# Channel fold from reflected sums, and a new order of the transfers at the layer boundary, in a two-layer encoder kernel

## The chip, the cores and the metric

The kernel runs on all 8 cores of one Trainium2 chip, one batch row (4096 positions of width 1024) on each core. No core talks to another. The metric is the device time in microseconds of the slowest core.

## The reference, cut to what matters

```
def fourier_mixer(h, w_in, w_out):              # layer 0
    proj = h @ w_in
    xin, z = proj[..., :E], proj[..., E:]       # E = 2048
    xg = xin.reshape(b, s, 8, 256)
    y = fft2(xg, axes=(positions, group channels), norm="ortho").real
    return (y.reshape(b, s, E) * silu(z)) @ w_out

def sgu_mixer(h, w_in, ...):                    # layer 1
    u, v = gelu(first 2E columns of h @ w_in);  z = the last E columns
    v = layer_norm(v); v = per chunk of 128 positions: w_s @ v + b_s
    return (u * v * silu(z)) @ w_out

for each layer:  x = x + mixer(rms_norm(x))
return rms_norm(x)
```

## The kernel before, in words

Layer 0 turns the order of the Fourier mixer round: the position transform is taken of the normed input (width 1024), and the channel transform is folded into the weights, so that one product per channel group gives the transformed branch. Layer 1 works on blocks of 512 positions.

**Opening (lines 446 to 521).** 32 steps, one tile of 128 positions each. SP loads x (`load_x`, up to 8 ahead in 6 buffers); ACT squares (`square`, L391); GpSimd makes the reciprocal root in two small operations (`norm`, L399 and L401); VectorE scales (L403); TensorE transposes (L481), applies the first part of the position transform (L491) and runs one group of gate columns (`zgroup`, L412, 8 matmuls). SP stores the intermediate U to DRAM. Two slices of fold weights (`load_wb`, 0 and 1) are loaded by GpSimd's queue in steps 12 and 14.

**Second transform (L551 to L584).** Eight steps `qd` from 7 to 0: SP has issued 32 loads of V; TensorE makes H (L558, L566), ACT and VectorE evict it (L545, L547). `fold(0)` runs in four parts, in steps 4 to 1. At the end GpSimd's queue issues loads of gate weights (`load_wz` 6 to 10) and fold weights.

**Groups g = 0 to 7 (L883 on).** `pq(g)` is 128 matmuls of 260 columns in eight steps, each evicted by ACT (`pc`, L269) and VectorE (L605, L608); `gate(g)` multiplies by the gate tiles `sz` (six of 8 KB a partition, used in turn) on VectorE (L626); `fold(g+1)` makes the weights `wp` for the next group; then `zall(zt)` makes further gate tiles, 64 matmuls each. A `tick()` after each of the 8 parts of `pq` and `zall` issues, by its count, a weight cast from DRAM to DRAM on GpSimd's queue (`casts`, 32 of 512 KB, the bf16 copies of layer 1's weights and of W0) or a store of a gated tile (`stores`, 1 MB on SP to `gy`). GpSimd's transfers cast f32 to bf16 on the way and land in the order of their queue.

`fold(g)` is, for each of 8 slices dc of the model width, two matmuls with 256 columns each, which add up over the two halves of the 256 group channels:

```
for kc in range(2):
    pe.op(lambda e: e.matmul(bank[:, h * 256:(h + 1) * 256],
                             wb[wb_slot(2 * g + kc)][0][:, dc * 128:(dc + 1) * 128], fmat[:, kc, :], ...
```

**Boundary (L907 to L980).** After the last `zall` SP loads the row tile `szsp`, W0 (two of 2 MB), three tiles of x (`load_x1`, 512 KB each) and `g1t` (512 KB). After `fold(6)` and `fold(7)`, `pq(6)` begins; `last_column` (L663) makes eight special rows, which GpSimd gates (L626 with GpSimd as its engine). SP then loads the even blocks of `gyt` (12 of the 16 channel blocks of the first 512 positions in two loads; blocks 12 to 15 are read from `sz` in place), stores the special rows (`gy<-szsp`), and loads the odd blocks. During `pq(7)` SP issues ring loads 1 to 4 (layer-1 weights, 1 MB each) and then ring 0, x tile 3 and the stores of blocks 12 to 15. TensorE goes on with `out0` (L751): 28 matmuls for position tile 0, 28 for tile 1, 4 for tile 0, and so on, 128 in all for the first block. `residual` and `norm1` follow for each tile, ACT transposes the normed tile by DMA (`send1`, L177) and `vtile` (L821) starts layer 1. From there on each 512-position block repeats the same 2-stage pattern: `vtile`, `wide` (L848) with `mix` (L858: four matmuls of 128 columns, each with weights of its own), `out1` and `out0` (L751).

The order on each engine is the order of the program text. An operation waits only for semaphores that a small dependency tracker (`Q.deps`) sets, also for buffers that share an address range.

Of the kernel before, what the change touches and what calls it, by code (L numbers as in the profile page):

```python
# [19 lines left out]

def _chan_order():
    o = []
    for g in range(8):
        o += [g * 256 + m for m in range(128)]
        o += [g * 256 + 128] + [g * 256 + 256 - m for m in range(1, 128)]
    return np.array(o)

def _host_consts():
    bf = ml_dtypes.bfloat16
    c = np.arange(256)[:, None]  # L30
    m = np.arange(128)[None, :]
    ang = 2 * np.pi * ((c * m) % 256) / 256.0
    Fm = np.concatenate([np.cos(ang), np.sin(ang)], axis=1)
    Fm[:, 128] = np.cos(np.pi * np.arange(256))
    Fm = Fm.reshape(2, 128, 256).transpose(1, 0, 2)
# [31 lines left out]
    pk = np.concatenate([Fm.reshape(128, 512), rows(B64)], axis=1)  # L67
# [115 lines left out]
def build():  # L183
# [9 lines left out]
    wb_in = din("wbT", [16, 128, D])  # L193
# [11 lines left out]
    c_pk = din("c_pk", [128, 576], BF16)  # L205
# [10 lines left out]
    with ExitStack() as es:  # L216
# [82 lines left out]
        with ExitStack() as sa:  # L299
# [11 lines left out]
            def tile(name, shape, dtype, off=None):  # L311
# [3 lines left out]
            cpk, cpkb = tile("cpk", [128, 576], BF16)  # L315
            tr, trb = tile("tr", [128, 128], BF16)
            fmat = cpk[:, 0:512].rearrange("p (a b) -> p a b", b=256)
            b64 = cpk[:, 512:576]
# [29 lines left out]
            wb = [tile(f"wb{i}", [128, D], BF16, (top["at"] - 4096 if i < 2 else vh + 2048 * (i - 2)) + 2048 * (i % 2 if i < 2 else 0))  # L348
                  for i in range(6)]
# [4 lines left out]
            wsT, wsTb = tile("wsT", [128, 8, 128], BF16)  # L354
            assert top["at"] <= nc.sbuf_usable_end, (top["at"], nc.sbuf_usable_end)
# [8 lines left out]
            d_wb = [dsem(f"d_wb{i}") for i in range(6)]  # L364
# [12 lines left out]
            def wb_slot(i):  # L377
                return i if i < 2 else 2 + (i - 2) % 4

            def load_wb(i):  # L380
                k = wb_slot(i)
                pool.dma(wb[k][0][:], wb_in[i], d_wb[k], writes=[wb[k][1]])
# [41 lines left out]
            def fold(g, dcs):  # L424
                w_, wpb = wp[g % 2]
                for d2 in dcs:
                    bank, bb = next_f()
                    for h in range(2):
                        dc = 2 * d2 + h
                        for kc in range(2):  # L430
                            pe.op(lambda e: e.matmul(bank[:, h * 256:(h + 1) * 256],  # L431
                                                     wb[wb_slot(2 * g + kc)][0][:, dc * 128:(dc + 1) * 128], fmat[:, kc, :],
                                                     start=(kc == 0), stop=(kc == 1)),
                                  [wb[wb_slot(2 * g + kc)][1], cpkb], [bb], waw=False, inc=(h == 1 and kc == 1))
# [30 lines left out]
            norm(2)  # L465
            zq = []
            behind = []
            nxt = 6
            for s in range(32):
# [38 lines left out]
                if s in (12, 14):  # L508
                    load_wb(s // 2 - 6)
# [16 lines left out]
            stores = []  # L526
            late = []

            def tick():
# [3 lines left out]
                if stores and ticks["n"] % 4 == 0:  # L533
                    stores.pop(0)()
# [16 lines left out]
            for qd in range(7, -1, -1):  # L551
# [34 lines left out]
            def pq(g):  # L586
                w_, wpb = wp[g % 2]
                (Dt, Dtb), (St, Stb) = DS[g == 7]
                for qd in range(8):
# [21 lines left out]
                    if g == 7 and 0 < qd < NR:  # L611
                        load_ring(qd)
# [197 lines left out]
            def send1(n):  # L810
                j_, jb = xn1[n % 2]
                t = n % 4
                act.dma_t(h1T[:, :, t * 128:(t + 1) * 128], j_[:], d_t[t], [jb], [h1Tb[t]])

            def vtile(i, t):
                sm_, smb = sm[t]
                for j in range(4):
                    r_, rb = ring[(12 * i + j) % NR]
# [22 lines left out]
            def wide(i, k, ct, func, out_ap, wb_):  # L841

                n = 12 * i + 4 + 4 * k + ct // 4
                r_, rb = ring[n % NR]
# [38 lines left out]
            for g in range(8):  # L883
                pq(g)
                if g == 0:
# [3 lines left out]
                    load_wz(11)  # L889
# [43 lines left out]
            sp.dma(gsp[6:8], g67[:, :], d_67, reads=[g67b], writes=gyTb[13:16:2], waw=True)  # L933
# [102 lines left out]
def _in_maps(inputs):  # L1036
# [7 lines left out]
    base["wbT"] = np.ascontiguousarray(w_in0[:, :E].T).reshape(16, 128, D)  # L1044
# [17 lines left out]
```

How the kernel before makes its waits and increments, by code:

```python
    def wait(self, tok):  # L105
        if tok is None:
            return
        sem, val = tok
        if sem is self.sem and self.kind == "pe":
            return
        k = id(sem)
        if self.seen.get(k, 0) >= val:
            return
        self.eng.wait_ge(sem, val)
        self.seen[k] = val
# [32 lines left out]
    def op(self, fn, reads=(), writes=(), waw=True, cost=0.3, inc=True):  # L148
        self.load += cost
        self.deps(reads, writes, waw)
        inst = fn(self.eng)
        if inc:
            self.n += 1
            inst.then_inc(self.sem, 1)
            tok = (self.sem, self.n)
        else:
            tok = (self.sem, self.n + 1)
        self.mark(tok, reads, writes, waw)
        return tok
# [1 line left out]
    def dma(self, out, in_, dsem, reads=(), writes=(), waw=False, more=False, **kw):  # L161
        if not more and dsem.n > 0:
            self.wait((dsem.sem, dsem.n))
        self.deps(reads, writes, waw)
        self.eng.dma_start(out=out, in_=in_, **kw).then_inc(dsem.sem, 16)
        dsem.n += 16
        tok = (dsem.sem, dsem.n)
        self.mark(tok, reads, writes, waw)
        return tok
# [1 line left out]
    def dma_t(self, out, in_, dsem, reads=(), writes=()):  # L172
        if dsem.n > 0:
            self.wait((dsem.sem, dsem.n))
        self.deps(reads, writes, True)
        self.eng.dma_start_transpose(out=out, in_=in_).then_inc(dsem.sem, 16)
        dsem.n += 16
        tok = (dsem.sem, dsem.n)
        self.mark(tok, reads, writes, True)
        return tok
```

## Time and profile before

| what | us |
|---|---|
| three runs | 1580.16, 1621.85, 1579.46 (median 1580.16) |
| the profiled execution, its own time | 1582.04 |
| its span on the slowest core (core 1) | 1580.7 |
| spans of the eight cores | 1564.3 to 1580.7 |
| TensorE busy on core 1 | 1545.7 |
| VectorE, ACT, GpSimd busy on core 1 | 747.1, 515.9, 156.4 |

The span runs from the first to the last instruction of a core; the execution's own time is 1.3 us longer. Busy times are sums over instructions, and matmuls are pipelined, so that the time of one is longer than the distance to the next.

### The profile page before, as it was taken

Reading aid. Unit: us, or ns where it says so; the run is one execution under the profiler, and the core shown is the slowest. Engines: PE = TensorE matmul, PEld = TensorE weight load, DVE = VectorE, ACT = ScalarE, POOL = GpSimd, SP = SyncE. Lnnn points to the kernel's source line nnn. Section 1 sums busy time; section 2 is a strip of 40 time slices with the busy share of each in tenths; the row PEclk is TensorE's granted clock in tenths of the full one; section 3 lists DMA queues with packets and bytes.
Section 4 is the critical chain, followed back from the end, with each engine's and each line's share of the span. In section 5 each row is a group of like instructions: output and inputs, shape, how many; then the busy total and the mean of one; then the engine's idle time right before and its main releaser. Section 6 shows DMA issues by size and latency. Waiting matters only on the chain.

```text
span 1580.7 us, 25439 instructions; the slowest of 8 cores (1564.3 to 1580.7 us)
## 1 busy us (share of the span) xinstructions
PE 1545.7 (98%) x8458; PEld 782.7 (50%) x8458; DVE 747.1 (47%) x1245; ACT 515.9 (33%) x915; POOL 156.4 (10%) x336
## 2 busy tenths in 40 slices
PE   6999999999899999999999999999999999999997
PEld 3557766646644444544444444445444444544443
DVE  5866532213636435624553463356245435624552
ACT  5766333333223313322331232133123313322331
POOL 3311111010211011001000100110010011001000
PEclk9999999999999999999999999999999999999999
DMA  9986999999887941643453155335324531643411
GB/s 256 288 249 170 171 139 152 152 144 180 250 205 189 242 176 48 226 150 98 152 199 125 38 188 199 107 116 201 134 69 167 207 113 47 226 152 96 148 46 54
DMA packets 103298, 247.72 MB, mean 157 GB/s; under 512 B 40042, under 2 KB 56042, under 8 KB 87402
## 3 DMA queue, kind: packets, MB, share of 16 engines
q1 hardware_dynamic: 53652, 207.76, 39.8%
q0 software_dynamic: 15568, 29.63, 14.9%
q10 hardware_dynamic: 33952, 8.72, 3.3%
q8 instruction: 71, 1.16, 0.3%
q14 instruction: 55, 0.45, 0.1%
HBM read 225.24 MB, written 58.87 MB: 180 GB/s over the span
## 4 chain that ended last, share of the span: by engine, by line
PE 94%; DMA 4%; DVE 1%; issue 1%; ACT 0%; SPq 0%; POOL 0%; DVEq 0%; ACTq 0%; POOLq 0%
PE pf L848 28%; PE pf L751 27%; PE pf L412 14%; PE pf L821 14%; PE pf L595 5%; PE pf L858 2%; DMA gy<-sz_77 1%; DMA a0x_59<-xt 1%; DMA gyt<-gy 1%; PE pb L481 1%; PE pf L491 1%; PE pf L558 1%; DMA h1T<-xn_0_2525 1%; PE pf L431 1%; SPq L166 0%
## 5 line engine op out<-in xcount | busy, mean ns | idle before, releaser
L751 PE MATMUL pf<-W_2513,gyt 128*128 128x512 bf16 x992 | 219.2, 382 | 7.4 <-DMA gyt<-gy 7.4
L751 PE MATMUL pf<-W_2524,u 128*128 128x512 bf16 x1024 | 222.3, 379 | 0.0
L751 PEld LDWEIGHTS pf<-W_2513,gyt 128*128 128x128 bf16 x992 | 97.6, 98 | 126.6 <-issue 13.0
L751 PEld LDWEIGHTS pf<-W_2524,u 128*128 128x128 bf16 x1024 | 100.2, 98 | 120.8
L851 ACT ACTIVATE u<-pf 128x512 bf16<-128x512 f32 x128 | 76.5, 597 | 164.2 <-PE pf L848 154.7
L825 ACT ACTIVATE v<-pf 128x512 f32<-128x512 f32 x128 | 75.4, 597 | 121.1 <-PE pf L821 101.6
L848 PE MATMUL pf<-h1T,ring_2522 128*128 128x512 bf16 x416 | 96.8, 385 | 0.0
L848 PE MATMUL pf<-h1T,ring_2519 128*128 128x512 bf16 x416 | 96.5, 382 | 0.0
L848 PE MATMUL pf<-h1T,ring_2523 128*128 128x512 bf16 x416 | 95.5, 380 | 0.0
L848 PE MATMUL pf<-h1T,ring_2520 128*128 128x512 bf16 x416 | 94.9, 379 | 0.0
L848 PE MATMUL pf<-h1T,ring_2521 128*128 128x512 bf16 x384 | 88.3, 379 | 0.0
L605 DVE TENSOR_TENSOR Dt_93<-pc_97,pf 128x256 bf16<-128x256 f32 x28 | 11.8, 421 | 144.9 <-PE pf L595 120.8
L862 DVE SCALAR_TENSOR_TENSOR ytmp_2532<-pf,gTs,TT 128x512 f32<-128x512 f32 x64 | 48.1, 751 | 48.6 <-PE pf L858 48.5
L742 POOL TENSOR_SCALAR sm_2546<-sm_2546 128x1 f32<-128x1 f32 x24 | 5.3, 221 | 631.6 <-ACT sqj L787 588.0
L848 PEld LDWEIGHTS pf<-h1T,ring_2522 128*128 128x128 bf16 x416 | 40.1, 99 | 44.4 <-issue 5.2
L848 PEld LDWEIGHTS pf<-h1T,ring_2523 128*128 128x128 bf16 x416 | 39.8, 98 | 43.8 <-issue 1.5
L848 PEld LDWEIGHTS pf<-h1T,ring_2519 128*128 128x128 bf16 x416 | 39.8, 98 | 43.6 <-issue 3.5
L848 PEld LDWEIGHTS pf<-h1T,ring_2520 128*128 128x128 bf16 x416 | 39.6, 98 | 43.3 <-issue 0.3
L851 ACT ACTIVATE sg_2543<-pf 128x512 bf16<-128x512 f32 x64 | 38.2, 598 | 69.2 <-PE pf L848 58.9
L851 ACT ACTIVATE sg_2544<-pf 128x512 bf16<-128x512 f32 x64 | 38.2, 598 | 67.6 <-PE pf L848 64.4
L595 PE MATMUL pf<-H,wp_85 128*128 128x260 bf16 x512 | 58.3, 276 | 0.0
L595 PE MATMUL pf<-H,wp_84 128*128 128x260 bf16 x512 | 57.6, 274 | 0.0
(298 smaller groups left out, 2317.8 us busy)
## 6 DMA issues: line engine op xcount, KB each, us to landing
ring_2519<-wind SPq DMA_DIRECT2D x20, 1024.0 KB, 7.4
ring_2520<-wind SPq DMA_DIRECT2D x19, 1024.0 KB, 7.1
ring_2521<-wind SPq DMA_DIRECT2D x19, 1024.0 KB, 6.7
ring_2522<-wind SPq DMA_DIRECT2D x19, 1024.0 KB, 7.1
ring_2523<-wind SPq DMA_DIRECT2D x19, 1024.0 KB, 6.4
gyt<-gy SPq DMA_DIRECT2D x7, 2048.0 KB, 12.4
wind<-w_in1p POOLq DMA_DIRECT2D x24, 512.0 KB, 42.1
V<-ud SPq DMA_DIRECT2D x32, 256.0 KB, 7.9
```

The costliest lines, as they stand in the source:

```text
L412: pe.op(lambda e: e.matmul(bank[:], w[:, dc, :], hT[:, dc, hb * 512:(hb + 1) * 512], start=(dc == 0), stop=(dc == 7)), [wb_, hTb[hb], hTal ...
L431: pe.op(lambda e: e.matmul(bank[:, h * 256:(h + 1) * 256], wb[wb_slot(2 * g + kc)][0][:, dc * 128:(dc + 1) * 128], fmat[:, kc, :], start=( ...
L481: pe.op(lambda e: e.transpose(out=bank[:, dc * 128:(dc + 1) * 128], in_=xn_[:, dc * 128:(dc + 1) * 128], identity=ident[:]), [xnb, identb] ...
L491: pe.op(lambda e: e.matmul(bank[:], tr[:], xn_[:, h * 512:(h + 1) * 512], start=True, stop=True), [trb, xnb], [bb], waw=False)
L595: pe.op(lambda e: e.matmul(bank[:, 0:HQ], w_[:, dc, cs * 128:(cs + 1) * 128], H[:, qd, dc, cs, :], start=(dc == 0), stop=(dc == 7)), [wpb, ...
L751: pe.op(lambda e: e.matmul(bank[:], lhs(kc), rhs[:, kc, nh * 512:(nh + 1) * 512], start=(kc == 0), stop=(kc == 15)), lb(kc) + rb(kc), [bb] ...
L821: pe.op(lambda e: e.matmul(bank[:], h1T[:, dc, t * 128:(t + 1) * 128], r_[:, dc, :], start=(dc == 0), stop=(dc == 7)), [h1Tb[t], rb], [bb] ...
L825: act.op(lambda e: e.activation(out=vj, in_=bank[:], func=AF.Gelu_apprx_tanh), [bb], [vjb])
L848: pe.op(lambda e: e.matmul(bank[:], r_[:, dc, c0:c0 + 128], h1T[:, dc, :], start=(dc == 0), stop=(dc == 7)), h1Tb + [rb], [bb], waw=False, ...
L851: act.op(lambda e: e.activation(out=out_ap, in_=bank[:], func=func), [bb], wb_)
L858: pe.op(lambda e: e.matmul(bank[:, t * 128:(t + 1) * 128], vhat[t][0][:, ct * 128:(ct + 1) * 128], wsT[:, ct // 2, :], start=True, stop=True),
L862: dve.op(lambda e: e.scalar_tensor_tensor(out=y_[:].rearrange("c (t p) -> c t p", p=128), in0=bank[:].rearrange("c (t p) -> c t p", p=128) ...
```

## The change: what it does

Two parts.

1. The fold uses the symmetry of cosine and sine. The host pairs channel c with 256 - c (row 0 pairs 0 with 128) and lays the f32 weights out in pieces: 8 groups of 4 quarters of the model width, 128 partitions, 2 x 256 values, 256 KB each. SP loads a piece without a cast into a staging buffer (`st`, one or two slots), and GpSimd makes the sum and the difference of its two halves as bf16 (`eo`), two operations of 128 x 256 a piece, 64 in all. The fold is then one matmul of 129 columns with the sums and one of 192 columns with the differences, in place of two of 256. Pieces 0 to 3 pass in steps 8 to 24 of the opening, 4 and 5 are loaded in steps 28 and 29, 6 to 11 pass in the second transform, and the generator `sums()` moves 12 to 31, one step a tick, six ticks a piece, through one slot. `eo` 1 and 2 lie where gate weights 0 to 3 lie, so `load_wz` 6 and 7 go behind `fold(1)` and 8 and 9 behind `fold(2)`. The other `load_wb` are gone.
2. At the boundary SP holds back the three x tiles and `g1t` until `gyt` has landed; the stores of blocks 12 to 15 each wait for one of the four transposes of `send1`; the ring's slots are turned by one, so that loads 0 to 3 go out during `pq(7)` and load 4 after it.

The diff, cut to its core:

```
+_HARM = [*range(0, 128, 2), *range(1, 128, 2)]
...
+    FE = np.concatenate([np.cos(ang), np.cos(np.pi * c)], axis=1)
+    FE[0, 64:128] = 0.0
+    FO = np.zeros((128, 192))
+    FO[0, :64] = 1.0
+    FO[1:, 64:] = np.sin(ang[1:])
...
+            eo = [tile(f"eo{i}", [128, 2, D], BF16, o) for i, o in enumerate((top["at"] - 4096, wzo, wzo + 4096, vh + 4096, vh))]
...
+            st = [tile("st0", [128, 2, 256], F32, top["at"] - 2048), tile("st1", [128, 2, 256], F32, top["at"] - 4160)]
...
+            def load_piece(n):
+                t_, b_ = st[n % 2 if 4 <= n < 12 else 0]
+                sp.dma(t_[:], wb_in[n // 4, n % 4], d_st[n % 2 if 4 <= n < 12 else 0], writes=[b_], waw=True)
+            def sum_piece(n):
+                t_, b_ = st[n % 2 if 4 <= n < 12 else 0]
+                eo_, eob = eo_of(n // 4)
+                q = n % 4
+                for k, op in enumerate((ALU.add, ALU.subtract)):
+                    pool.op(lambda e: e.tensor_tensor(out=eo_[:, k, q * 256:(q + 1) * 256], in0=t_[:, 0, :],
+                                                      in1=t_[:, 1, :], op=op), [b_], [eob], waw=False)
+            folded = {"n": 0, "summed": 12}
+            def sums():
+                for n in range(12, 32):
+                    while n >= 20 and folded["n"] < n // 4 - 1:
+                        yield
+                    load_piece(n)
+                    for _ in range(4):
+                        yield
+                    sum_piece(n)
+                    folded["summed"] += 1
+                    yield
+                    yield
...
+                while folded["summed"] < 4 * g + 4:
+                    next(summing)
...
-                        for kc in range(2):
-                            pe.op(lambda e: e.matmul(bank[:, h * 256:(h + 1) * 256],
-                                                     wb[wb_slot(2 * g + kc)][0][:, dc * 128:(dc + 1) * 128], fmat[:, kc, :],
-                                                     start=(kc == 0), stop=(kc == 1)),
+                        for k, f, a, z in ((0, fE, 0, 129), (1, fO, 64, 256)):
+                            pe.op(lambda e: e.matmul(bank[:, h * 256 + a:h * 256 + z], eo_[:, k, dc * 128:(dc + 1) * 128], f,
+                                                     start=(k == 0), stop=True, skip_group_check=(k == 1)),
...
-                    if 0 < g < 6:
-                        load_wb(2 * g + 4)
-                        load_wb(2 * g + 5)
+                    folded["n"] = g + 1
...
-                if s in (12, 14):
-                    load_wb(s // 2 - 6)
+                if s in (12, 16, 20, 24):
+                    sum_piece(s // 4 - 3)
+                if s in (8, 12, 16, 20):
+                    load_piece(s // 4 - 2)
+                if s in (28, 29):
+                    load_piece(s - 24)
...
+            keep = {"n": 0}
...
+                next(summing, None)
+                if len(stores) > keep["n"] and ticks["n"] % 4 == 0:
                     stores.pop(0)()
...
+                for n in ((4,), (5, 6), (7,), (8,), (9,), (10,), (11,), ())[7 - qd]:
+                    sum_piece(n)
+                    if n < 10:
+                        load_piece(n + 2)
                 if qd == 0:
-                    load_wb(2)
-                    load_wb(3)
-                    for i in range(6, 9):
-                        load_wz(i)
-                    load_wb(4)
-                    load_wb(5)
-                    for i in range(9, 11):
-                        load_wz(i)
+                    load_wz(10)
...
                     if g == 7 and 0 < qd < NR:
-                        load_ring(qd)
+                        load_ring(qd - 1)
...
-                    k = n % NR
+                    k = (n + 1) % NR
...
                 act.dma_t(h1T[:, :, t * 128:(t + 1) * 128], j_[:], d_t[t], [jb], [h1Tb[t]])
+                if n < 4:
+                    sp.wait((d_t[t].sem, d_t[t].n))
+                    stores.pop(0)()
+                    if n == 3:
+                        sp.dma(gsp[6:8], g67[:, :], d_67, reads=[g67b], writes=gyTb[13:16:2], waw=True)
...
-                    load_wz(11)
+                    for i in (6, 7, 11):
+                        load_wz(i)
...
                 if g == 7:
-                    load_ring(0)
                     load_x1(3)
-                if g == 7:
-                    while stores:
-                        stores.pop(0)()
+                    load_ring(4)
...
+                if g == 1:
+                    for i in (8, 9):
+                        load_wz(i)
...
-                    for n in range(3):
-                        load_x1(n)
-                    sp.dma(g1t[:], g1.partition_broadcast(128), d_g1, writes=[g1b], waw=True)
...
                 if g == 6:
+                    keep["n"] = 4
...
                     sp.dma(gyt[:, 1:12:2, :], even[1, :, 0:6, 0:512], d_g, reads=gyTb[1:12:2], writes=[gytb], more=True)
+                    sp.wait((d_g.sem, d_g.n))
+                    for n in range(3):
+                        load_x1(n)
+                    sp.dma(g1t[:], g1.partition_broadcast(128), d_g1, writes=[g1b], waw=True)
```

## Rows read from the trace of the kernel before

**Rows 1.** The page: its head, and busy time by engine.
```profile
span 1580.7 us, 25439 instructions; the slowest of 8 cores (1564.3 to 1580.7 us)
PE 1545.7 (98%) x8458; PEld 782.7 (50%) x8458; DVE 747.1 (47%) x1245; ACT 515.9 (33%) x915; POOL 156.4 (10%) x336
```

**Rows 2.** Span and granted clock by core: core 3.
```profile
core 3: 1578.8 us, clock 0.990
```

**Rows 3.** Waits of TensorE on core 1: us in total, times, longest.
```profile
PE pf L751 <- DMA gyt<-gy: 7.4, 1, 7.4
```

**Rows 4.** Stretches of core 1: length, busy by engine, clock, DMA share, GB/s.
```profile
75.00:85.00 10.00, 10.00 (x72) 5.42 (x71) 9.47 (x13) 8.14 (x16) 2.91 (x7) 1.00 1.01 318
...
151.00:388.00 237.00, 237.00 (x1511) 147.75 (x1510) 70.78 (x231) 80.98 (x162) 34.48 (x55) 1.00 1.04 150
```

**Rows 5.** Chain that ended last, in order of time: start, us, what.
```profile
164.94 1.75 PE pf L431 x16
...
449.81 10.68 DMA h1T<-xn_0_2525
...
501.82 1.73 PE pf L848 x8
503.77 1.73 PE pf L848 x8
...
548.70 55.25 PE pf L751 x256
```

**Rows 6.** Timeline of core 1, 385 to 465 us: start, us, engine, line.
```profile
394.63 0.33 SPq L166 DMA_DIRECT2D gy<-sz_77  x1
...
398.74 8.73 POOL L626 TENSOR_TENSOR szsp<-p_100,szsp 8x2048 bf16<-8x2048 f32 x4 [53.16 <-ACT pc_97 L269]
...
407.22 14.35 PE L595 MATMUL pf<-H,wp_85 128*128 128x260 bf16 x128
...
413.38 0.29 SPq L166 DMA_DIRECT2D gy<-szsp  x1
...
415.91 0.39 SPq L166 DMA_DIRECT2D gyt<-gy  x1
...
428.92 4.57 PE L751 MATMUL pf<-W_2513,gyt 128*128 128x512 bf16 x12 [7.35 <-DMA gyt<-gy]
...
460.84 1.89 PE L821 MATMUL pf<-ring_2519,h1T 128*128 128x512 bf16 x8 [1.21 <-DMA h1T<-xn_0_2525]
```

**Rows 7.** Core 3: the last matmuls of `pq`, and the first of `vtile`.
```profile
405.96 14.35 PE L595 MATMUL pf<-H,wp_85 128*128 128x260 bf16 x128
...
L821 PE MATMUL pf<-ring_2519,h1T x224: 379/379/379, 455.7 to 1478.4; 128*128 128x512 bf16 x112
```

**Rows 8.** Transfers issued at 380 to 386 us: KB each, us to landing.
```profile
x_0_2515<-x SPq DMA_DIRECT2D x1, 512.0 KB, 17.9
...
g1t<-l_norm SPq DMA_DIRECT2D x1, 512.0 KB, 20.4
```

**Rows 9.** Groups by shape: GpSimd's largest product.
```profile
L626 POOL TENSOR_TENSOR szsp<-p_100,szsp 8x2048 bf16<-8x2048 f32 x1 | 4.1, 4072 | 53.2 <-ACT pc_97 L269 53.2
```

**Rows 10.** Timeline of core 1 near the opening's end.
```profile
98.57 0.57 POOL L401 TENSOR_TENSOR stats<-stats,mhalf 128x1 f32<-128x1 f32 x1 [0.21 <-POOL stats L399]
...
99.31 0.75 DVE L403 TENSOR_SCALAR a0xn_63<-a0x_55,stats 128x1024 bf16<-128x1024 f32 x1
...
101.34 0.61 PE L481 MATMUL pb<-ident,a0xn_63 128*128 128x128 bf16 x8
```

**Rows 11.** Transfers issued at 44 to 50 us, then at 166 to 172 us, to landing.
```profile
a0x_55<-xt SPq DMA_DIRECT2D x1, 512.0 KB, 7.2
...
wz_83<-wz POOLq DMA_DIRECT2D x1, 256.0 KB, 37.6
```

**Rows 12.** Stores and loads of SP: beside the casts, and in layer 1.
```profile
gy<-sz_73 SPq DMA_DIRECT2D x1, 1024.0 KB, 20.0
...
x_0_2515<-x SPq DMA_DIRECT2D x7, 512.0 KB, 3.7
```

More of the change, by code:

```diff
@@ L23, in _chan_order @@
     for g in range(8):
-        o += [g * 256 + m for m in range(128)]
-        o += [g * 256 + 128] + [g * 256 + 256 - m for m in range(1, 128)]
+        o += [g * 256 + m for m in _HARM]
+        o += [g * 256 + 128] + [g * 256 + 256 - m for m in _HARM[1:]]
     return np.array(o)
@@ L29, in _host_consts @@
     bf = ml_dtypes.bfloat16
-    c = np.arange(256)[:, None]
-    m = np.arange(128)[None, :]
+    c = np.arange(128)[:, None]
+    m = np.array(_HARM)[None, :]
     ang = 2 * np.pi * ((c * m) % 256) / 256.0
-    Fm = np.concatenate([np.cos(ang), np.sin(ang)], axis=1)
-    Fm[:, 128] = np.cos(np.pi * np.arange(256))
-    Fm = Fm.reshape(2, 128, 256).transpose(1, 0, 2)
+    FE = np.concatenate([np.cos(ang), np.cos(np.pi * c)], axis=1)
[3 more added lines that the diff above has]
+    FO[1:, 64:] = np.sin(ang[1:])
     TR = np.zeros((128, 2, 2, 32))
@@ L65, in rows @@
         return a.reshape(4, 32, -1).transpose(1, 0, 2).reshape(128, -1)
-    pk = np.concatenate([Fm.reshape(128, 512), rows(B64)], axis=1)
+    pk = np.concatenate([FE, np.zeros((128, 1)), FO, rows(B64)], axis=1)
     bdt = np.stack([rows(BD[pr]) for pr in range(32)], axis=1)
@@ L313, in tile @@
                 return t, Buf(name, (o, o + n))
-            cpk, cpkb = tile("cpk", [128, 576], BF16)
+            cpk, cpkb = tile("cpk", [128, 386], BF16)
             tr, trb = tile("tr", [128, 128], BF16)
-            fmat = cpk[:, 0:512].rearrange("p (a b) -> p a b", b=256)
-            b64 = cpk[:, 512:576]
+            fE = cpk[:, 0:129]
+            fO = cpk[:, 130:322]
+            b64 = cpk[:, 322:386]
             g0s, g0sb = tile("g0s", [128, 8], F32)
@@ L347, in build @@
             wp = [tile(f"wp{i}", [128, 8, 256], BF16) for i in range(2)]
-            wb = [tile(f"wb{i}", [128, D], BF16, (top["at"] - 4096 if i < 2 else vh + 2048 * (i - 2)) + 2048 * (i % 2 if i < 2 else 0))
-                  for i in range(6)]
+            eo = [tile(f"eo{i}", [128, 2, D], BF16, o) for i, o in enumerate((top["at"] - 4096, wzo, wzo + 4096, vh + 4096, vh))]
             bdt, bdtb = tile("bdt", [128, 32, 128], BF16, top["at"])
@@ L363, in build @@
             d_wz = [dsem(f"d_wz{i}") for i in range(6)]
-            d_wb = [dsem(f"d_wb{i}") for i in range(6)]
+            d_st = [dsem(f"d_st{i}") for i in range(2)]
             d_gy = [dsem(f"d_gy{i}") for i in range(6)]
@@ L375, in load_wz, with eo_of @@
                 pool.dma(wz[i % 6][0][:], wz_in[i], d_wz[i % 6], writes=[wz[i % 6][1]])
[L377 to L382, printed above, removed]
+            def eo_of(g):
+                return eo[g if g < 3 else 4 - g % 2]
+            def load_piece(n):
[20 more added lines that the diff above has]
+                    yield
             def load_x(t):
@@ L465, in build @@
             norm(2)
+            summing = sums()
             zq = []
@@ L532, in tick @@
                     next(casts, None)
-                if stores and ticks["n"] % 4 == 0:
+                next(summing, None)
+                if len(stores) > keep["n"] and ticks["n"] % 4 == 0:
                     stores.pop(0)()
@@ L817, in vtile @@
                 for j in range(4):
-                    r_, rb = ring[(12 * i + j) % NR]
+                    r_, rb = ring[(12 * i + j + 1) % NR]
                     bank, bb = next_f()
@@ L843, in wide @@
                 n = 12 * i + 4 + 4 * k + ct // 4
-                r_, rb = ring[n % NR]
+                r_, rb = ring[(n + 1) % NR]
                 c0 = (ct % 4) * 128
@@ L1043, in _in_maps @@
     base["wz"] = np.ascontiguousarray(wz.transpose(2, 1, 0, 3))
-    base["wbT"] = np.ascontiguousarray(w_in0[:, :E].T).reshape(16, 128, D)
+    c = np.arange(128)
+    pairs = np.stack([c, np.where(c > 0, 256 - c, 128)])
+    wb = w_in0[:, :E].T.reshape(8, 256, 4, 256)[:, pairs]
+    base["wbE"] = np.ascontiguousarray(wb.transpose(0, 3, 2, 1, 4))
     base["w_out0p"] = np.ascontiguousarray(f32["l0_w_out"][order].reshape(16, 128, D).transpose(1, 0, 2))
```

8 lines of the change are left out of this document (4 added, 4 removed).

## The prediction

> **What bounds the kernel now.** I read the page's head first: TensorE is busy in 1545.7 of 1580.7 us, and no other engine in half of that [rows 1]. The time is TensorE's instructions at their pitch plus some 35 us in which it has none, so an edit counts only if it shortens TensorE's stream or closes one of its gaps. The spans by core come second: the metric is the slowest core, and core 3 is within 2 us of core 1 [rows 2], so both have to be followed. Third, TensorE's waits: the long one outside the first steps is for `gyt<-gy`, 7.4 us, once [rows 3], at the boundary of the layers. Fourth, stretches: from 151 to 388 us TensorE is busy all the time while the DMA engines are busy all the time too (share 1.04, much of it casts), and in the opening both TensorE (10.00 of 10) and VectorE (9.47 of 10) are full [rows 4]. The chain and the timeline give the prices.
>
> **The fold.** One group's fold is 16 matmuls of 256 columns in 1.75 us: 109.4 ns each [rows 5]. For the narrower ones I need the pitch at other widths. Between two groups of `wide` stand four matmuls of 128 columns with weights of their own; the groups start 1.95 us apart and take 1.73 [rows 5], which leaves 0.22 / 4 = 55 ns. So a column costs (109.4 - 55) / 128 = 0.425 ns; 129 columns take 55.4 and 192 columns 82.2. A pair falls from 218.8 to 137.6 ns, 81.2 ns less; with 64 pairs 5.2 us. Seven of the eight folds stand in the stretch where TensorE never waits, so 4.5 us of it is certain if the pitch is; the eighth (0.65 us) lies among evictions and may vanish. ACT's evictions of the fold stay as they are, beside the gate matmuls.
>
> The Trainium skill speaks against this (TensorE: Matmul & The Clock Gate, Back-to-back issue gap): in a stream of weight loads and matmuls it gives about 81 ns a matmul at 128 columns, because the load counts too. By it the 129-column matmul would take 81 ns, and the fold would save about 3.5 us. The 55 ns of this kernel's own pairs [rows 5] disagree, so I stay with 5.2.
>
> **The boundary.** On core 1 the last `pq` matmul ends at 407.22 + 14.35 = 421.57; the 128 matmuls of `out0` take 27.63 (half of 55.25 for 256 [rows 5]), so layer 1 could start at 449.2. It starts at 460.84 [rows 6]: 11.6 us are lost, 7.35 waiting for `gyt`, 1.21 for the first transpose, and the rest in matmuls at a low clock behind the gap (the first 12 took 4.57 us, where 12 at full pitch are 2.6). On core 3 the same sum is 405.96 + 14.35 + 27.63 = 447.9 against 455.7 [rows 7]: 7.8 us.
>
> Does the new order close the gap? The odd half of `gyt` is issued at 415.91, behind the store of the special rows, which goes at 413.38 because it waits for the store issued at 394.63 [rows 6]. From 381 to 413 us SP's queue moved W0 (4 MB), three x tiles and `g1t` (2 MB) and two stores (2 MB): 8 MB in 32 us. x and `g1t` took 18 to 20 us to land [rows 8]. Without their 2 MB the store lands 8 us earlier, at 405.4. Then GpSimd's gating of the special rows is last, 398.74 + 8.73 = 407.5 [rows 6]; 2.5 us for the store, and the odd half goes out at 410. Its landing took 12.5 us with three ring loads behind it (415.91 to 428.4); 0.75 MB at 8 MB in 32 us is 3 us, and 3.7 us was the price of a quiet 512 KB load [rows 12]. So it lands at 414 to 422.5, against 421.6: a wait of 0 to 1 us. I take 0, by the nearer, quiet row.
>
> What is late next: the x tiles and `g1t` leave SP behind its new wait for `gyt`, at 415, and behind them ring loads 0 to 4 and x tile 3. 2 MB at that rate is 8 us, so they land by 423; even from 422.5 they land by 431. The first sum with x comes 60 matmuls into `out0`, at 421.6 + 13.0 = 434.6. The first ring tile (4 us behind) is needed at 449. The first transpose was issued at 449.81, 20.9 us after `out0` began, and took 10.68 [rows 5]; from 421.6, and with 2 to 3 us of slow matmuls gone, it goes at about 440 and at the old price lands at 451, 2 us late. But the stores of blocks 12 to 15 (4 MB) no longer run beside it, so I take 0 and keep 2. The stores, each behind a transpose on SP, free `sz` for `vhat` and the tables, which come 7 us and more into `vtile`; behind SP's waits stand only the special rows of groups 6 and 7, `bsB` and later ring loads, not needed before `vtile` ends, 27.6 us on.
>
> **What the pieces cost.** GpSimd's largest product has 2048 elements in 4.07 us, 1.99 ns an element [rows 9]; 256 elements are 0.51 us, and the fixed part lies below the 0.57 of a one-element root [rows 10]: 0.5 to 1.1 us each, 32 to 70 us in all on an engine that is 10% busy. In the groups and in the second transform TensorE needs them long after. In the opening they are near the path: the pair (1.0 to 2.2 us) follows the root on GpSimd, and the next root stands behind it. At 98.57 the root, at 99.31 VectorE's scaling (done 100.06), at 101.34 the transposes [rows 10]: 1.3 us of slack. Four pairs push four roots by 0 to 0.9 us beyond that, 0 to 3.6 us. Also `load_piece(1)` makes SP wait for the first sum: about 7 us of late x loads. A load landed 7.2 us after issue [rows 11], six or more steps of 2.6 us (15 us) ahead: hidden. Together I take 1 us, bounds 0 to 5. The 20 later pieces on SP and the 14 casting fold loads that go move the same 256 KB each way of SBUF; I book nothing either way.
>
> The Trainium skill adds a mechanism here (SBUF — State Buffer, Who interferes with whom): GpSimd and VectorE share a port pair, and the later instruction blocks until the other ends, for a VectorE scaling as for a product of two SBUF inputs. By it eight sums hold up a VectorE that is 95% busy, some 5 us in the opening, and the result would be 1570. No row of this trace shows such a meeting in the opening, and my upper bound of 5 holds it already.
>
> **The sum.** Core 3: 1578.8 - 5.2 - 7.8 + 1.0 = 1566.8. Core 1: 1580.7 - 5.2 - 11.6 + 1.0 = 1564.9. So core 3 becomes the slowest, 13.9 us below the old span. The profiled execution took 1582.04 us in all; the median of the runs shown is 1580.16, 1.9 lower, and against it the forecast is **1566.3 us**, 0.9% less.
>
> **Rivals.**
> *The wait only changes its name* (1576, chance 0.14): the gap closes for `gyt`, and the transposes, x tiles or ring loads, all later now, cost the 7 to 12 us instead. For it: landing times of 18 to 20 us in this stretch [rows 8]. Against: 4 MB of stores move out of it. Then only the fold's 5.2 less 1 us remains.
> *Gate weights land late* (1584, chance 0.08): loads 6 and 7 go behind `fold(1)` and are needed after two gate groups, `pq(1)` and `fold(2)`, 3.5 + 14.35 + 1.1 = 19 us on. A load issued there landed after 37.6 us [rows 11], behind casts; then TensorE stands 18 us. Against: nine casting loads that were ahead of those casts are gone from that moment.
> *The pieces come late; slower than before* (1586, chance 0.06): one staging slot means load, sum, load in turn. 20 pieces have 237 us, 11.8 each; the pair takes 1.3, so it decides when the mean landing passes 10.5 us, and each us above costs 20 us of TensorE's wait at the last folds. A 1 MB store there took 20.0 us, a quiet 512 KB load 3.7 [rows 12]. If five pieces stand behind pairs of stores (20 us) and 15 take 5, the mean is 8.8: in time. At 11.5 the kernel is at 1586; at 13 it is at 1616, over 2% slower.
> *The fold gets no cheaper* (1571.5, chance 0.05): the weight loads set the pitch, and only the boundary counts.
>
> **How the numbers follow.** The forecast has 0.67. Its own range is 1561 (no cost in the opening; the eighth fold counts) to 1573 (5 us in the opening, 2 at the transpose). The range for 8 in 10 reaches to the second rival, 1584, and below to 1558, 5 us under the 1563.4 that core 1's full gain would give, since core 3's clock of 0.990 is worth up to 1% and need not stay. Only the piece rival with landings above 12.8 us passes 2% (31.6 us; about what a measurement can tell from no change): 0.05 slower. A gain of 2% exceeds all gaps that this change touches: 0.01. Within 2%: 0.94.
>
> **What would show it.** Right: fold groups of about 1.1 us; no wait of TensorE for `gyt`; `vtile` starting 13 to 17 us earlier, near 444 on core 1, with the clock near 1.00 there. Wrong: waits of TensorE on `eo` (GpSimd) or `wz` in the groups, an opening that ends more than 1 us later, TensorE waiting for `h1T`, x or ring tiles at 435 to 450 us.

## The result and the profile after

The changed kernel takes 1572.36 us (median of four runs, 1570.57 to 1572.63) beside 1580.81 for the kernel before: a ratio of 0.9947, 95% interval 0.9927 to 0.9967. Ratios compare fast runs alone and leave out slow ones, here the 1621.85 of one run of the kernel before. The forecast was 1566.3, its own range 1561 to 1573, and "within 2%". The total lies just inside that range, 6 us above the point, and two errors of opposite sign sit inside it. In the ratio 0.5% were gained where 0.9% were forecast.

The page of the changed kernel, its head and the busy times by engine:

```profile
span 1570.9 us, 25586 instructions; the slowest of 8 cores (1560.2 to 1570.9 us)
...
PE 1535.5 (98%) x8458; PEld 778.1 (50%) x8458; DVE 751.3 (48%) x1245; ACT 514.7 (33%) x915; POOL 199.2 (13%) x384
```

Against [rows 1] TensorE is busy for 10.2 us less and GpSimd for 42.8 more (core 7 here, core 1 there): the 64 sums and differences take 52.0, and 16 casting loads fewer to issue give 8.4 back. Alone a sum takes 0.72 to 0.73; ten of the 64 take 1.2 to 1.7. Span and granted clock by core:

```profile
core 0: 1568.3 us, clock 0.995
core 1: 1560.2 us, clock 0.998
core 2: 1565.4 us, clock 0.997
core 3: 1562.1 us, clock 0.997
...
core 5: 1567.3 us, clock 0.997
...
core 7: 1570.9 us, clock 0.994
```

Cores 1 and 3, on which the forecast was worked out, end at 1560.2 and 1562.1 instead of 1564.9 and 1566.8. Core 7, the fastest before (1564.3), is now the slowest. So what the forecast did on two cores has to be done on all of them. I cut each span at four starts that TensorE's rows show (first matmul of the second transform, first of `pq`, last of `pq`, first of `vtile`):

| stretch | before, core 1 | after, core 1 | before, core 7 | after, core 7 |
|---|---|---|---|---|
| opening | 116.0 | 115.5 | 114.1 | 119.0 |
| second transform | 34.6 | 34.6 | 34.6 | 34.6 |
| first to last `pq` | 270.7 | 266.4 | 269.6 | 273.4 |
| last `pq` to `vtile` | 39.5 | 27.7 | 29.9 | 27.7 |
| `vtile` to the end | 1119.8 | 1116.0 | 1116.0 | 1116.2 |

On core 7 the boundary gave 2.2 us, the groups took 3.8 and the opening 4.8: so it ends 6.6 us later than before.

**The boundary closed.** The chain of core 1, in order of time (start, us, what):

```profile
394.94 21.83 PE pf L631 x197
416.77 27.63 PE pf L787 x128
444.40 25.68 PE pf L862 x119
```

`pq`, `out0` and `vtile` follow each other without a piece of anything else between them, where before stood the wait of [rows 3], the slow matmuls of [rows 6] and the transpose of [rows 5]. All eight cores read like this (27.7 us).

**The groups gave back what the fold saved.** TensorE's waits on core 1 and on core 7, in their own views (a fold's matmuls are L466, their eviction to `wp` L474, the gate matmuls L444):

```profile
PE pf L631 <- ACT wp_84 L474: 1.0, 1, 1.0
```
```profile
PE pf L444 <- DMA wz_78<-wz: 4.9, 1, 4.9
```

The second is the rival "gate weights land late". Its chain on core 7:

```profile
153.77 14.19 PE pf L631 x128
167.96 1.14 PE pf L466 x16
...
169.72 22.83 DMA wz_78<-wz
...
192.79 22.40 PE pf L444 x94
```

GpSimd and TensorE on core 7 around it, in the timeline:

```profile
156.92 2.74 POOL L172 DMA_DIRECT2D w0d<-w_out0p  x4
...
169.72 0.59 POOL L172 DMA_DIRECT2D wz_78<-wz  x1 [8.62 <-PE pf L466]
...
186.56 1.29 PE L466 MATMUL pf<-cpk,eo_88 128*128 128x129 bf16 x16
192.79 15.93 PE L444 MATMUL pf<-hT,wz_78 128*128 128x512 bf16 x64 [4.93 <-DMA wz_78<-wz]
```

Four casts go out at 156.9, the gate weights 13 us behind them on the same queue; 18 us after that they are needed, and they land after 22.8. The 64 matmuls behind the wait take 15.9 us; at their usual pitch of 1.73 us for 8 they are 13.8. The granted clock in the stretches shows why:

```profile
190.00:195.00 5.00, 2.21 (x6) 0.85 (x7) 4.56 (x6) 0.00 (x0) 2.35 (x4) 0.50 1.01 161
195.00:200.00 5.00, 5.00 (x21) 2.06 (x20) 0.30 (x1) 1.19 (x2) 0.00 (x0) 0.82 0.95 132
200.00:205.00 5.00, 5.00 (x25) 2.27 (x24) 0.00 (x0) 1.79 (x3) 1.40 (x2) 1.00 1.10 234
```

(clock third from the right: 0.50, that is 1.2 GHz, from 190 to 195 us, in which TensorE still stood until 192.8; between the two levels from 195 to 200, and 1.00, that is 2.4 GHz, from 200 on). The wait costs 7.0 us in all on core 7: 273.4 where the undisturbed cores have 266.4. In the same way cores 0, 2 and 5 pay 4.2 to 6.7; cores 1, 3, 4 and 6 nothing. The same load on core 3, and on core 7:

```profile
wz_78<-wz POOLq DMA_DIRECT2D x1, 256.0 KB, 7.4
```
```profile
wz_78<-wz POOLq DMA_DIRECT2D x1, 256.0 KB, 22.8
```

So landings differ by 15 us between cores, around a margin of 18, and the metric takes the worst of eight.

### The profile page after: what moved, and what is told of

It reads as the page before. It is cut to its first block, busy times and chain, and to the rows that moved or that the text cites. A ratio compares the mean times of both kernels' runs of the same rounds, so it can differ in the third digit from the quotient of the medians.

```text
span 1570.9 us, 25586 instructions; the slowest of 8 cores (1560.2 to 1570.9 us)
## 1 busy us (share of the span) xinstructions
PE 1535.5 (98%) x8458; PEld 778.1 (50%) x8458; DVE 751.3 (48%) x1245; ACT 514.7 (33%) x915; POOL 199.2 (13%) x384
## 4 chain that ended last, share of the span: by engine, by line
PE 93%; DMA 3%; issue 1%; DVE 1%; ACT 1%; POOL 0%; DVEq 0%; ACTq 0%; POOLq 0%; SPq 0%
PE pf L787 28%; PE pf L889 28%; PE pf L862 14%; PE pf L444 13%; PE pf L631 6%; PE pf L899 2%; DMA wz_78<-wz 1%; DMA a0x_54<-xt 1%; DVE hT L517 1%; PE pf L597 1%; PE pb L514 1%; PE pf L524 0%; PE pf L466 0%; DVE H L586 0%; POOL stats L433 0%
## 5 line engine op out<-in xcount | busy, mean ns | idle before, releaser
L787 PEld LDWEIGHTS pf<-W_2568,gyt 128*128 128x128 bf16 x992 | 97.1, 98 | 116.8
L641 DVE TENSOR_TENSOR Dt_92<-pc_96,pf 128x256 bf16<-128x256 f32 x28 | 11.8, 420 | 145.3 <-PE pf L631 117.9
```

The costliest lines, as they stand in the source:

```text
L787: pe.op(lambda e: e.matmul(bank[:], lhs(kc), rhs[:, kc, nh * 512:(nh + 1) * 512], start=(kc == 0), stop=(kc == 15)), lb(kc) + rb(kc), [bb] ...
```

## The experiments

All are compared with the kernel before on the same chip. The first four ran on one chip, the next seven on a second, the last on a third.

**1. The casts held back.** The theory on record: what is missing to the forecast is the queue order, four casts ahead of `wz` 6 and 7.

```
-                if ticks["n"] % 4 == 1:
+                if ticks["n"] % 4 == 1 and ticks["n"] > 8:
...
                 if qd == 0:
                     load_wz(10)
-                    for _ in range(2):
-                        next(casts, None)
```

> The changed kernel, with the first four casting transfers of GpSimd's queue held back until the second gate group begins, so that gate-weight loads 6 and 7 lead that queue. Theory (the late gate weights are the queue's order): TensorE's wait for wz at the seventh gate group goes on every core (it was 2.6 to 4.9 us on cores 0, 2, 5 and 7), load 6 lands within 10 us of its issue everywhere, the stretch from the first to the last pq falls to 266.4 us on all eight cores (it was 270.6 to 273.4 on those four), and the slowest core is at about 1564 us of span, some 1565 in time: ratio to the kernel before about 0.990. Rival (the DMA engines are loaded, by the 1 MB store and the pieces, whatever the order): waits of 2 us and more stay on at least two cores, load 6 still takes 15 us, and the time stays at 1569 or above.

Measured: 1.0006 (0.9995 to 1.0017), 1584.0 us. The cause was right: the wait for `wz` is gone on all cores, and load 6 lands in 3.7 to 5.2 us on the eight cores (in the changed kernel 7.4 to 22.8). The time was 19 us above the expected one. On core 5, TensorE's waits and GpSimd's timeline:

```profile
PE pf L785 <- DMA gyt<-gy: 19.6, 1, 19.6
```
```profile
380.79 2.72 POOL L172 DMA_DIRECT2D wind<-w_in1p  x4
```

The loop spends one cast every fourth tick, so four were left over at the fifth group and went out in one go at 381 us, beside W0, the stores and `gyt`. The boundary took 36.3 to 49.4 us on the eight cores instead of 27.7. The wait was moved, not removed.

**2. The opening without its sums.** The kernel leaves the first channel group out of the output; a memset, not shown, fills its weights with zeros. It was run once (1571.1 us), so only its stretches are read.

```
...
-                if s in (12, 16, 20, 24):
-                    sum_piece(s // 4 - 3)
```

> The changed kernel without the four pairs of sums and differences on GpSimd in the first transform; their loads stay, and the even and odd rows of group 0 are zeros, so the first channel group is left out of the output. Theory (the sums push roots, and with them VectorE's scalings and the transposes): the first matmul of the second transform starts at 114.7 us in the mean over cores, as in the kernel before, against 117.0 in the changed one; the steps after a sum take 2.6 us instead of 2.9 to 3.0. Rival (the loads of pieces and what they push on SP's queue cost it, the stores and V loads late): the mean stays at 116 or above. If it comes out between, at 115.5 to 116, both have a share.

The opening ended at 115.5 in the mean over the cores. On the same chip the two other kernels that have the four sums (experiments 1 and 4) had 116.8, and the one with the old opening (experiment 3) 115.4. So the four pairs cost 1.3 us, and nothing is left over for the loads. My expectation had compared with profiles from other chips: between chips the opening differs by more than that (the last section has the numbers).

**3. and 4. The two parts alone.** The kernel before with the hunks of part 2; and the changed kernel with those hunks taken out.

> The kernel before with the second part of the change alone (order of the entry transfers, ring one slot on, stores of blocks 12 to 15 behind the transposes); the fold is the old one. Theory (the parts are independent): no wait for gyt or h1T, out0 in 27.6 us straight behind the last pq on every core; that takes 11.8 us from core 1, 6.9 from core 0, 8.5 from core 3, 2 to 11.5 from the others. With the clock loss of 4 to 7 us that die 0 showed behind the boundary in the kernel before, cores 2 and 3 end last at about 1570 us of span; without it 1566. Time 1567 to 1571.5, ratio 0.991 to 0.994. Rival (the gap closed only because the casting fold loads are gone too): a wait for gyt of 3 us or more stays on some core and the time is at 1574 or above.

> The changed kernel with the old boundary: the fold by sums and differences alone. Theory (the fold saves 3.2 us of TensorE, the opening costs 2 and late gate weights up to 7, the slowest core decides): the wait for wz stands on three or more cores, the wait for gyt of 5 to 8 us is back, and the time is 1579 to 1585, ratio 0.999 to 1.003: the fold as it was put in gains nothing. By the forecast's own sum it would be 1576 (5.2 less 1), ratio 0.997.

The boundary alone: 0.9909 (0.9891 to 0.9927), 1567.4 us. The fold alone: 1.0010 (0.9995 to 1.0025), 1585.3. Seven cores of the first show the gap closed or nearly so (27.7 to 29.2 us); on core 1, with 33.8, something is left:

```profile
PE pf L827 <- DMA h1T<-xn: 2.9, 1, 2.9
PE pf L752 <- DMA gyt<-gy: 2.8, 1, 2.8
```

The changed kernel has neither, which fits the rival. That the old fold's casting loads are the reason isn't shown: experiment 10 keeps them, moves eight casts away, and closes the gap on all cores. In the second kernel the groups last 266.4 to 274.1 us (269.6 on every core of the first). Core 4 waits 5.65 us at the gate weights again, where load 6 took 23.2, and core 1 waits 3.9 for a gate tile (`sz`) that is still being stored. As it was put in, the fold gains nothing; the whole gain is the boundary's. Both kernels take 1116.0 to 1116.2 us behind the boundary on all cores.

**5., 6. and 7. Two other places for the four casts.** In 5 I took away the burst at the fifth group and issued the rest of the casts in layer 1; in 6 four extra casts make up for the held ones:

```
-                if ticks["n"] % 4 == 1 and ticks["n"] > 8:
+                if ticks["n"] % 4 == 1 and ticks["n"] > 8 or ticks["n"] in (43, 51, 67, 75):
```

7 is 5 with two edits more: `st[n % 2]` for the pieces of the opening too, and `fold(6)` in `pq(5)`.

> The changed kernel with the first four casts held back as before, and the four that are then left over at the fifth gate group issued in layer 1, behind the first tile of vtile. Theory (the first hold-back lost at the boundary because four casts, some 2 MB of writes and twice that of reads, ran beside W0, the stores and gyt): no wait for wz and none for gyt over 1 us, the stretch from the first to the last pq 266.4 us on all cores, spans of 1560 to 1564.5, time about 1565, ratio 0.989 to 0.991. Rival (holding casts back makes the pieces or stores late in itself): the wait for gyt stays above 5 us on half the cores and the time is at 1572 or above.

> The changed kernel with the first four casts held back and made up by four extra ones between the 43rd and the 75th step of the gate groups, so that none is left at the fifth. Theory: as with the leftover behind the boundary, no wait for wz or gyt; but this stretch's DMA engines are busy all the time, so pieces and stores land later there: 1564 to 1569, with single waits of 1 to 3 us for sz or eo on some core. Rival (the stretch has no room for four more): a wait for eo or sz over 3 us on two or more cores, and 1572 or above.

> The leftover casts behind the boundary, and two edits more: the opening's pieces go into two staging slots in turn, so that SP never waits for a sum, and the fold of group 6 stands after the sixth step of pq(5), so that ScalarE's evictions of it have 3.6 us of TensorE work beside them. Expected: the wait of 1.0 us of pq(6) for wp goes; the stretch from the first to the last pq is 265.4; the first matmul of the second transform comes at 117.0 in the mean as in the changed kernel if SP's wait costs nothing (the forecast's step), at 116 if it costs; time 1563 to 1565, ratio 0.988 to 0.990.

5 gave 1.0027 (0.9994 to 1.0060), 6 gave 1.0011 (0.9982 to 1.0040), 7 gave 1.0010 (0.9988 to 1.0032). None waits for `wz`. Experiment 5 was not what its text says: `pq(5)` and `pq(6)` have ticks of their own, nothing on GpSimd held the casts, and the first of them went out at 365 to 374 us. On core 3:

```profile
373.98 2.71 POOL L172 DMA_DIRECT2D wind<-w_in1p  x4
```
```profile
428.10 5.28 PE L785 MATMUL pf<-W,gyt 128*128 128x512 bf16 x12 [10.39 <-DMA gyt<-gy]
```

So 5 and 7 repeat experiment 1 in a milder form (boundary 30.6 to 41.2 us). Experiment 6 has no casts there and its boundary takes 27.7 to 28.5 us: the casts were the cause. But four cores waited 5.7 to 10.0 us among the four `zall` ahead of `pq(5)`. Core 2, waits, then SP and ACT in the timeline:

```profile
PE pf L444 <- ACT sz L448: 10.0, 1, 10.0
```
```profile
308.20 36.89 SPq L172 DMA_DIRECT2D st<-wbE  x4
345.29 1.00 SPq L172 DMA_DIRECT2D gy<-sz  x2
...
362.30 3.04 ACT L448 ACTIVATE sz<-pf 128x512 bf16<-128x512 f32 x6 [18.94 <-DMA gy<-sz]
```

Read from the bottom: ACT could not write the gate tile because its old content was still being stored; the stores went out at 345 because SP stood behind four pieces for 37 us, each of which waits for the sum of the one before. The changed kernel has the same chain, a little shorter, on the same core:

```profile
299.53 32.56 SPq L172 DMA_DIRECT2D st_99<-wbE  x4
```

There a piece of this stretch landed after 6.9 us in the median, here after 10.2. This is the chain of pieces from the third rival, but it delays stores, not the fold.

Of 7's two edits, the wait for `wp` went (groups 265.7 to 266.4), and two staging slots gained nothing: the opening ended at 115.7, at 115.4 in 5. SP's wait for the sums is hidden, as forecast.

**8., 9. and 10. Casts truly behind the boundary.** No cast after the 117th tick (8), the 101st (9) or the 85th (10); the rest stands behind the memset that waits for the last `pq`:

```
-                if ticks["n"] % 4 == 1:
+                if ticks["n"] % 4 == 1 and 8 < ticks["n"] <= 120:
...
                     if i == 0 and t == 1:
                         sp.dma(bsB[:], ...)
+                        for _ in casts:
+                            pass
```

9 has `fold(6)` in `pq(5)` too; 10 is the boundary part alone, old fold, with the same eight casts behind.

> The changed kernel with 28 casts in the gate groups, from the ninth step on, and the last four truly behind the boundary: the earlier attempt let GpSimd issue its four leftover casts at 370 us, at once behind the fifth group, and they ran beside the boundary all the same. Theory (each late transfer is one of what stands ahead of it: casts ahead of wz, casts beside gyt): no wait for wz, no wait for gyt over 1 us, first to last pq 266.4 us, spans 1559 to 1565, time about 1565; ratio some 0.006 below the changed kernel's in the same session. Rival (the four held casts are needed out of the way in any case, and the gate stores behind SP's piece waits decide): waits for sz of 5 us and more on two or more cores, and a time no better than the changed kernel's.

> As the last, with eight casts behind the boundary instead of four (the last in the groups at the 101st step) and the fold of group 6 within pq(5). Theory: the stores and pieces of the last groups land earlier too; no wait for wz, gyt, sz or wp; first to last pq 265.5 us; time 1562 to 1565, ratio 0.988 to 0.991. Rival (eight casts beside layer 1's first ring loads and transposes make those late): TensorE waits for h1T or ring, 3 us or more, and nothing is gained on four.

> The kernel before with the boundary's part alone and the last eight casts behind the boundary; the old fold. Theory: the gap of 3.0 us that was left on one core goes, out0 follows pq on all, first to last pq 269.6 us: 3.2 more than the new fold, but the opening comes 1.5 earlier; spans 1561 to 1565, time 1565 to 1566.5. If the new fold, freed of its late transfers, is worth anything, this is 1 to 3 us slower than e9; if it comes out equal or faster, the fold as it was put in is worth nothing here.

8 gave 1.0062 (1.0040 to 1.0084), 9 gave 1.0162 (1.0146 to 1.0178), 10 gave 1.0164 (1.0142 to 1.0186). Up to `vtile` everything is as the theory said on every core (8: 266.4, then 27.7; 9: 265.7 to 265.8, then 27.7). Behind it, `vtile` to the end takes 1128 to 1132 us in 8 and 1144 to 1153 in 9 and 10, instead of 1116.1. Core 5 of 8:

```profile
PE pf L887 <- DMA ring<-wind: 6.3, 1, 6.3
PE pf L785 <- DMA W<-w_out1p: 4.2, 1, 4.2
```

The last rival had named the ring; neither side had named W1 (`W`): its four casting loads stand behind the casts on the same queue. On core 2 they took 56.5 us to land in the median, in the changed kernel 36.4. 10, with the old fold, pays the same, so this is the casts' price: 14 us for four and 32 for eight. Up to `vtile` the new fold of 9, with nothing late, is 2.7 us ahead of the old one of 10 (443.0 against 445.7 in the mean over the cores, its longer opening counted): that is what it is worth when its transfers stand in nobody's way.

**11. The changed kernel again,** beside these three.

> The changed kernel once more, as it is, beside the three others on the same chip. Expected: a ratio of 0.993 to 0.998, the wait for wz on two to five of the cores, out0 straight behind pq on all.

0.9964 (0.9949 to 0.9979), 1566.05 us, spans of 1558.7 to 1563.9. My expectation of two to five waits missed: load 6 took 7.0 to 18.1 us here, just within the margin of 18, and TensorE waited under 1 us at the gate weights on every core; core 6 waited 2.9 for `sz`. The 1566 is the forecast's number by chance: beside it the kernel before runs at 1572.4 (1575.7 beside experiments 5 to 7 on the same chip), and the gain is 0.36%, where 0.9% was forecast.

**12. The casts earlier.** On core 7 of the changed kernel the DMA engines are 0.36 to 0.44 busy from 140 to 160 us. So the four go there, with `fold(6)` in `pq(5)`:

```
...
+                if qd == 5:
+                    for _ in range(4):
+                        next(casts)
...
```

> The changed kernel with the same number of casts before the boundary, none of them moved later: the first four go earlier, behind the seventh piece's sums in the second transform, where the DMA engines were 0.36 to 0.44 busy from 140 to 155 us on core 7; and the fold of group 6 stands in pq(5). Theory (a cast costs by what stands behind it, and this is the one stretch with room): the four are issued at 141 to 147 us instead of 149 to 157 and are done before the gate-weight loads, which land within 12 us on every core; no wait for wz, none for gyt, none for wp; first to last pq 265.6 us, post-boundary 1116.1; spans 1558 to 1563, time 1560 to 1565 and 0.004 to 0.006 in ratio below the changed kernel. Rival (the pieces and V loads pay for it): the second transform takes over 35.5 us, or a wait for eo of 2 us and more stands at the third fold, and nothing is gained.

0.9995 (0.9985 to 1.0005), 1573.8 us. No wait for `wz`, but the groups last 274.5 to 275.9 us on all eight cores. Core 1, waits, then GpSimd and ACT in the timeline:

```profile
PE pf L632 <- ACT pc L275: 7.4, 1, 7.4
```
```profile
155.75 1.40 POOL L397 TENSOR_TENSOR eo<-st 128x256 bf16<-128x256 f32 x2 [8.88 <-DMA st<-wbE]
160.45 1.40 POOL L397 TENSOR_TENSOR eo<-st 128x256 bf16<-128x256 f32 x2 [3.31 <-DMA st<-wbE]
...
161.95 0.67 ACT L275 ACTIVATE pc<-pf 128x260 f32<-128x260 f32 x2 [11.52 <-POOL eo L397]
```

The second staging slot lies on the memory of `pc`. Beside the casts the last pieces take 7.6 us in the median to land instead of 2.7 to 2.9 (changed kernel, core 1), so that the slot comes free at 162, and until then ACT can't evict `pq(0)`.

## Why the prediction was right or wrong

**The boundary: right, in size and way.** "11.6 us are lost" on core 1: 11.8 were. "`vtile` near 444": 444.2. No transpose, x tile or ring load took the place of the wait; the 2 us kept for the transpose were not needed. Experiment 3 shows that this holds by itself, up to one core's 6 us.

**The fold's pitch: right; its effect: mis-sized.** A group takes 1.14 us (forecast 55.4 and 82.2 ns a pair: 1.10). The Trainium skill (TensorE: Matmul & The Clock Gate, Back-to-back issue gap) gives about 81 ns a matmul at 128 columns; by it the group would be 1.3, an estimate. The trace has 71 ns in the mean over both widths, so the kernel's own rows decided rightly. Of 5.2 us, 3.2 arrived (269.6 to 266.4): seven groups at 1.14 instead of 1.75 are 4.3, and 1.0 goes back. The mis-sized step is "ACT's evictions of the fold stay as they are, beside the gate matmuls": folds 6 and 7 stand back to back, with no gate matmuls, and TensorE now waits 1.0 us for ACT; experiment 7 takes it away. The eighth fold's 0.65 vanished among the evictions, as it said it might (34.6 us both times). On core 3 that stretch got longer instead, 36.2; at its end:

```profile
146.00:152.00 6.00, 5.14 (x34) 2.79 (x35) 2.94 (x8) 3.28 (x9) 4.47 (x7) 0.72 0.48 131
```

The clock is 0.72 in the mean there, and the last eight gate matmuls take 3.36 us where eight take 1.89 earlier in the stretch. Twelve of the 88 core profiles with the new fold have 35.2 to 36.2 us in this stretch, none of the 24 with the old one. Why the clock falls on those cores isn't shown.

**The opening: right in size, by another way.** 1 us was taken, 1.3 was found in the mean of eight cores (experiment 2). The step at 79 us on core 7 shows how; GpSimd, VectorE and TensorE in the timeline:

```profile
79.11 0.61 PE L514 MATMUL pb<-ident,a0xn_62 128*128 128x128 bf16 x8
...
79.47 0.73 POOL L397 TENSOR_TENSOR eo_86<-st_99 128x256 bf16<-128x256 f32 x1
...
79.68 1.07 DVE L435 TENSOR_SCALAR a0xn_63<-a0x_59,stats 128x1024 bf16<-128x1024 f32 x1
80.16 1.18 POOL L397 TENSOR_TENSOR eo_86<-st_99 128x256 bf16<-128x256 f32 x1
...
81.85 0.57 POOL L433 TENSOR_TENSOR stats<-stats,mhalf 128x1 f32<-128x1 f32 x1 [0.21 <-POOL stats L431]
82.03 0.61 PE L514 MATMUL pb<-ident,a0xn_63 128*128 128x128 bf16 x8 [0.16 <-DVE hT L517]
...
82.59 0.75 DVE L435 TENSOR_SCALAR a0xn_60<-a0x_54,stats 128x1024 bf16<-128x1024 f32 x1
```

The first sum takes its usual time. The scaling, begun while it runs, takes 1.07 instead of 0.75 and ends 0.55 after it; the second sum takes 1.18 and ends 0.58 after the scaling. The step takes 2.92 instead of 2.6, and four such steps are 1.2 to 1.3 us. The forecast's own way, a pair that pushes the next root, is hidden in this step: that root ends at 82.42, and VectorE is busy until 82.48. The other mechanism, which it had named and kept out of its number, is what the step shows. The Trainium skill (SBUF — State Buffer, Who interferes with whom) lets the first comer keep the shared ports for its whole instruction while the other waits. The rows above agree: the first sum is not stretched, and each later instruction ends behind the one before it. Only the forecast's price for it, 5 us for eight sums, was too high: the scaling meets one sum a step and loses 0.3.

On core 7 the opening lost 4.8 us against the profile before, not 1.3. 3.8 of them were lost by the eighth step, at 33.4 us, when the first piece had only just been asked for (32.5): that is not the work of the sums. Why the first steps of this core were slow in this execution stays open.

**Gate weights: the rival, and the forecast's real error.** It had the place and the margin right (19 us there, 18 in the trace) and a chance of 0.08. The point against it, "nine casting loads that were ahead of those casts are gone" (eight are; load 10 stays), looked at loads ahead of the casts; what counts is the four casts ahead of the load, and they had stayed. The wrong turn is to ask how long a load takes on one core: landings spread from 7.4 to 22.8 us over eight cores around a margin of 18, and the slowest sets the time. Four profiles have this order (the result, experiments 2, 4 and 11); in three of them some core waits 4.9 to 5.7 us. A chance of 0.08 was far too low.

**What came back unasked, and luck in the total.** The forecast took over a loss that is no part of the change: behind the boundary cores 0 to 3 took 1119.8 to 1123.1 us in the profiled execution of before, and 1116.0 to 1116.2 in the changed one; experiment 4, with the old boundary, has 1116.0 to 1116.2 too. TensorE had no wait there, but its granted clock fell in single stretches, on these four cores alone. Core 3 of before:

```profile
495.00:505.00 10.00, 10.00 (x56) 4.90 (x55) 6.95 (x10) 2.63 (x5) 0.00 (x0) 0.91 1.02 216
```

Why it fell in that execution stays open. Without the loss, 3.8 us on core 1 and 7.1 on core 3, the same sum gives 1561.1 for core 1 as the slowest, 1560.6 in time: 12 us under the measured median and outside the forecast's own range. So that the total came within the range is luck: what went away by itself made up for about half of what the gate weights, core 7's first steps and the smaller gain of the fold took.

**Can the wait be avoided?** Five places for the four casts were tried, and something came late behind each:

| the four casts | what came late | lost |
|---|---|---|
| 148 to 159 us, as changed | `wz` 6 | 4.2 to 7.0, four cores of eight; under 1 in experiment 11 |
| 140 to 144 (12) | pieces, so `pc` | 6.7 to 7.9 (wait), all cores |
| 43rd to 75th tick (6) | pieces, so stores, so `sz` | 5.7 to 10.0 (wait), four cores |
| 364 to 387 (1, 5, 7) | `gyt` | 3 to 22, all cores |
| 460 to 466 (8) | W1, ring | 12 to 16, all cores |

No version ran that is shown to beat the changed kernel. The boundary part alone has the lowest ratio (0.9909, 0.9891 to 0.9927, on the first chip). The changed kernel has 0.9947 and 0.9964, but the two were not run side by side, and the ratio depends on the chip, so which is faster stays open. What was not tried is a slot for `eo` 1 elsewhere than on gate weights 0 and 1, which would let loads 6 and 7 lead the queue without moving a cast.

## What to carry to other kernels

Of five places for the same transfers none was free, not even the one where the DMA engines were 0.36 to 0.44 busy. Before you move a transfer, write down for each queue at its new place what stands behind it, which memory that shares, and with how much slack. Where the metric is the slowest of eight cores, weigh a margin against the spread of landings, not their median: a wait that half the cores run into sets the time. And where a change has two parts, time each alone; here one carried the whole gain.

## What the runs showed of the hardware

The queue of casting transfers takes more of the DMA engines' time than the bytes that the profile counts for it suggest. The page of the changed kernel, queues (packets, MB, share of 16 engines' span):

```profile
q1 hardware_dynamic: 58260, 216.10, 41.7%
q0 software_dynamic: 13264, 25.43, 12.5%
```

That is 0.49% a MB for GpSimd's queue (q0) and 0.19% on q1. At 166 to 172 us on core 1, while load 6 was under way there:

```profile
q0 software_dynamic: 371, 0.70, 101.5%
```

The packets of 0.70 MB took all the time of 16 engines, at 117 GB/s; in the opening of the kernel before the share was 1.01 too, at 318 GB/s [rows 4]. So GB/s alone do not tell whether a stretch is full, and a cast counts by its time. The second thing I had not expected is how much the same instructions differ between chips: the old opening ended at 114.8, 115.4 and 113.8 us in the mean over the cores in three profiles. The new one ended at 116.7 and 116.8 in two profiles of the first chip and at 115.0 to 115.7 in six of the second, so chips differ by as much as the edit under study moved it.
